# Query blocks 2, 3, 6 and 7 of the expert layers: other buffers, another load order, and four instead of six row gathers ahead

## The chip, the cores and the metric

The program runs on one core of one Trainium2 chip. The metric is the device time of one execution in microseconds (us). Engines are named as in the profile: PE (TensorE), DVE (VectorE), ACT (ScalarE), POOL (GpSimd) and SP (SyncE, which here only issues transfers). A block, a gather or one head's keys are 128 x 2048 f32, that is 1,048,576 bytes, called 1 MB or one unit below.

## What is computed

Two transformer blocks one after the other, 256 tokens of width 1024, in f32. The first block has two layers, and each ends in the same expert stage, which is where the change lies:

```
def peer_ffn(h, w_query, sub_keys, expert_u, expert_v):
    q = (ht @ w_query).reshape(T, Hh, 2, PEER_HALF)          # 256 x 1024 @ 1024 x 2048
    scores = jnp.einsum('thpd,hpkd->thpk', q, sub_keys)
    s_top, i_top = lax.top_k(scores, K)                      # 16 of 128, twice
    cand = s_top[:, :, 0, :, None] + s_top[:, :, 1, None, :]
    best, pos = lax.top_k(cand, K)                           # 16 of 256
    expert_idx = ...; gates = softmax(best)
    u = expert_u[idx]                                        # 8 heads x 16 picks a token
    a = gelu(einsum('tkd,td->tk', u, xb)) * gates
    return einsum('tk,tkd->td', a, expert_v[idx])
```

For each token and each of 128 picks one row of `u` and one of `v` (1024 f32 each) are read from a table in memory. The picks depend on the data, so these rows are gathered.

## The kernel before

**The stages.** Retention mixer, expert layer 0, gated mixer (`sgu`), expert layer 1, then the second block (hybrid attention, memory attention, MLP). Everything is written out by hand: each engine runs its own list in program order, and the lists are tied by semaphores.

**Weight blocks.** Every weight matrix is cut into blocks of 128 x 4 x 512. SP issues their loads one after the other in the order of one long list (`for i in range(limit)`), most of them into a ring of `R = 4` buffers. Before a load SP waits until PE has used the block that held the buffer last (`wait_block_free`: `w_used`, or `sum_ready` where that block was the last of a product). While SP waits, all that is behind it in the list waits too. ACT makes the rounded high part of a block (`ring_high`, L2117) and DVE the rest (`ring_low`, L1293), in place over the raw block; PE multiplies the three terms.

**The query product** of an expert layer has eight blocks, here called b0 to b7: b0, b1 for column group 0, b2, b3 for group 1, b4, b5 for group 2, b6, b7 for group 3. b8, b9 are the first two of the next matrix (`sgu_w_in` in layer 0, `w_kv_mem` in layer 1). b4 and b5 have buffers of their own (`early_scores`, `early_mod`), the others go through the ring. So b6 and b7 wait for b0 and b1 to be used, b8 and b9 for b2 and b3. Groups 0 and 1 are multiplied before the first pick is applied; groups 2 and 3 are cut into pieces and put between the picks.

**The gathers.** Two tiles of 128 tokens, 128 picks each: 256 gathers a layer, picks s = 0 to 255. One gather (POOL, L569) brings for each of 128 tokens the row pair u, v of its pick into a slot of 8 KB a partition. There are nine slots: 0 to 5 in the arena (`uv0` to `uv5`, from offset 8192 on, 2048 apart), 6 and 7 in the upper half of `ring_high` (`uv_high`), 8 is `spare`. `pick_slots` deals them out: eight at first, slot 5 from pick 68 on (`OPEN_AT`). Pick s waits until the pick that had its slot before is used (`uv_used`). DVE then multiplies u with the token (`dot`, L1705), ACT makes the gate a diagonal matrix (`p_diag`), PE adds the gated v (L1025).

**The first picks.** `choose_first` gives the first eight indices of head 0 early (`first_idx_ready`). Slots 6 and 7 lie on high parts of b2 and b3, so POOL waits ahead of pick 6 for the product of group 1 (`sum_ready` of `("query", l, 1)`):

```
if s == 6:
    pool.wait_ge(sum_ready, SUM[("query", l, 1)] + 1)
```

POOL's list is in order, so all gathers behind pick 6 wait there too.

Of the kernel before, what the change touches and what calls it, by code (L numbers as in the profile page):

```python
# [8 lines left out]
F32 = mybir.dt.float32  # L9
F32R = mybir.dt.float32r  # L10
# [14 lines left out]
RET_HEADS = 4  # L25
# [9 lines left out]
PICKS = PEER_HEADS * TOPK  # L35
# [7 lines left out]
R = 4  # L43
RH = 4
BN = 512
BK = 4
# [7 lines left out]
OPEN_AT = 68  # L54
# [45 lines left out]
def pick_slots():  # L100


    opened = 2 * [{0: (0, 1, 2, 3, 4, 8, 6, 7), OPEN_AT: (5,)}]
    at, before, held = [], [], {}
    for l in range(2):
        free, row, old = collections.deque(), [], []
        for s in range(TT * PICKS):
            free.extendleft(reversed(opened[l].get(s, ())))
            slot = free.popleft()
            free.append(slot)  # L110
            row.append(slot)
            old.append(held.get(slot))
            held[slot] = l * TT * PICKS + s
        at.append(row)
        before.append(old)
    return at, before
# [69 lines left out]
def two_blocks(nc, w, out):  # L186
# [10 lines left out]
    SMALL = small_in_order()  # L197
# [18 lines left out]
    limit = len(blocks)  # L216
    kv_first = first_block_of[("mem_kv", 0)]
    query_first = [first_block_of[("query", l, 0)] for l in range(2)]
    paired = {i for l in range(2) for i in range(query_first[l] + 4, query_first[l] + 10)} | set(range(kv_first, kv_first + 10))
    high_at = [i % 2 if i in paired else i % RH for i in range(limit)]  # L220
    early = {query_first[l] + 4 + e: R + e for l in range(2) for e in range(2)}
    raw_at, in_ring = [], 0
    for i in range(limit):
        raw_at.append(early[i] if i in early else in_ring % R)
# [9 lines left out]
    with ExitStack() as ctx:  # L234
        def sb(name, shape, dt=F32):
            return ctx.enter_context(nc.sbuf_tensor(name, shape, dt))

        def sem(name):
            return ctx.enter_context(nc.semaphore(name))
# [10 lines left out]
        ring_low = nc.alloc_sbuf_tensor_at("ring_low", [P, R, BK, BN], F32R, offset=ring_base)  # L250
        high_base = (nc.sbuf_base + 31) // 32 * 32
        ring_high = sb("ring_high", [P, RH, BK, BN], F32R)
        spare = sb("spare", [P, 2, D])
        x = sb("x", [P, TT, D])
        gain_base = (nc.sbuf_base + 31) // 32 * 32
# [35 lines left out]

        early_raw = [at("early_scores", 6144, BK, BN), nc.alloc_sbuf_tensor_at("early_mod", [P, BK, BN], F32, offset=mod_base + 12288)[:]]
        early_low = [at("early_scores_low", 6144, BK, BN, dt=F32R), nc.alloc_sbuf_tensor_at("early_mod_low", [P, BK, BN], F32R, offset=mod_base + 12288)[:]]
        raws = [ring[:, i] for i in range(R)] + early_raw
        raw_lows = [ring_low[:, i] for i in range(R)] + early_low

# [48 lines left out]
        small = [ctx.enter_context(nc.psum_tensor(f"small{i}", [P, 512], F32)) for i in range(2)]  # L345


        w_in = [sem(f"w_in{i}") for i in range(R + 2)]
        w_high, w_low, w_low_pool = sem("w_high"), sem("w_low"), sem("w_low_pool")
        t_high = sem("t_high")  # L350
        w_used = sem("w_used")
# [2 lines left out]
        small_ready = sem("small_ready")  # L354
# [25 lines left out]
        dot_ready, diag_ready, uv_used = sem("dot_ready"), sem("diag_ready"), sem("uv_used")  # L380
# [110 lines left out]
        def norm_count(n, t):  # L491
            return TT * NORM[n] + t + 1
# [18 lines left out]
        @block.sync  # L511
        def _(sp):
            sp.dma_start(col[:], w["cols"]).then_inc(c_in, 16)
            for k in range(KD):
                sp.dma_start(first_rows[k].rearrange("p a d -> p (a d)"), w["ada_w"][0, k * P:(k + 1) * P, 0:2 * D]).then_inc(first_in[k], 16)
                if k == 1:
                    sp.dma_start(x[:], w["x"][0].rearrange("(t p) d -> p t d", p=P)).then_inc(x_in, 16)
                    sp.dma_start(ident[:], w["ident"]).then_inc(cst_in, 16)
            for i in range(limit):
                if raw_before[i] is not None:  # L520
                    wait_block_free(sp, raw_before[i])
                if i in early:
                    l = query_first.index(i - 4 - early[i] + R)
                    if early[i] == R:
                        sp.wait_ge(sum_ready, SUM[("sgu_out", 1) if l else ("ret_out", 1)] + 1)
                    else:
                        sp.wait_ge(h_ready, h_count(1 + 2 * l, 1, 1))
                if i in behind_rows:
                    sp.wait_ge(dot_ready, behind_rows[i])
                sp.dma_start(raws[raw_at[i]], blocks[i]).then_inc(w_in[raw_at[i]], 16)  # L530
                for j in loaded_after[i]:
                    if j == 6 * KD:
                        sp.wait_ge(x_ready, norm_count(2, 1))
                    load_ada(sp, j)
            for t in range(TT):
                sp.wait_ge(out_ready, t + 1)
                sp.dma_start(out[0, t * P:(t + 1) * P, :], f_out[:, t, :]).then_inc(out_done, 16)
            sp.wait_ge(out_done, 16 * TT)
# [3 lines left out]
        def _(pool):  # L542
# [3 lines left out]
            def gathers(l):  # L546

                for s in range(TT * PICKS):
                    if s == 0:
                        pool.wait_ge(first_idx_ready, l + 1)  # L550
                    elif s == TOPK // 2 or s % TOPK == 0:
                        pool.wait_ge(idx_ready, l * UNITS + s // TOPK + 1)
                    if s == OPEN_AT:
                        pool.wait_ge(small_ready, SMALL[("scores", l, 3, TT - 1)] + 1)
                        if l == 0:
                            pool.dma_start(s_wsT, w["ws_turned"]).then_inc(ws_in, 16)
                    if l == 1 and s == 5 * TOPK:
                        load_gain(mix_gain, w["g_mix_2"], mix_gain_in)
                        pool.dma_start(b_mask, w["att_mask"]).then_inc(hyb_in, 16)
                        pool.dma_start(b_ga, bc(w["g_attn_out_2"].rearrange("(a d) -> a d", a=1), [P, 512])).then_inc(hyb_in, 16)  # L560
                    if l == 1 and s == PICKS + TOPK:
                        pool.wait_ge(dot_ready, TT * PICKS + PICKS)
                        load_gain(final_gain, w["norm_final"], gain_in[0])
                    if s == 6:
                        pool.wait_ge(sum_ready, SUM[("query", l, 1)] + 1)
                    if SLOT_BEFORE[l][s] is not None:
                        pool.wait_ge(uv_used, SLOT_BEFORE[l][s] + 1)
                    k = s % PICKS
                    nc.gpsimd.indirect_dma_start(uv_rows[SLOT[l][s]].rearrange("p a d -> p (a d)"), None, experts,  # L569
                                                 bass.IndirectOffsetOnAxis(ap=p_idx[:, k:k + 1], axis=0))\  # L570
                        .then_inc(landed[l, s][0], 16)
# [2040 lines left out]
```

## Time and profile before

| | |
|---|---|
| time, median of 3 runs | 2240.28 us (2239.32 to 2241.86) |
| the profiled execution | 2242.59 us, its span 2240.8 us |
| PE busy | 1973.3 us (88%) |
| DVE busy | 1561.9 us (70%) |
| ACT busy | 1029.4 us (46%) |
| POOL busy | 623.7 us (28%) |
| moved by DMA | 761.24 MB, mean 340 GB/s |
| of it by the gathers' queue (q0) | 548.94 MB |

The span is the time from the first to the last instruction of the profiled execution; the time also holds the 1.8 us around it. Busy shares are means over stages with different limits. "DMA share" is the mean busy share of the 16 DMA engines. An engine's "idle" is followed by what ended it.

### The profile page before, as it was taken

What the parts mean: (1) busy time and instruction counts of PE and PEld (TensorE: products, weight loads), DVE (VectorE), ACT (ScalarE), POOL (GpSimd) and SP (SyncE); (2) the same over time, 40 slices, a digit from 0 to 9 for tenths busy, and PEclk for the clock granted to TensorE, in tenths of its full rate; (3) what the DMA queues carried; (4) which work ended last, traced back from release to release, by engine and by line L of the source; (5) the groups of instructions that cost most, each with busy time, mean ns of one, the idle gap of its engine ahead of it and who ended that gap; (6) DMA issues with size and microseconds to landing.
All of it is one profiled execution on the core that took longest, in us unless ns stands there. A gap on an engine that the chain in (4) does not pass through costs nothing. (4 is left out here: it accounts for less than half of the span.)

```text
span 2240.8 us, 24068 instructions
## 1 busy us (share of the span) xinstructions
PE 1973.3 (88%) x8100; PEld 1242.8 (55%) x8100; DVE 1561.9 (70%) x2944; ACT 1029.4 (46%) x2171; POOL 623.7 (28%) x552
## 2 busy tenths in 40 slices
PE   6999899977778888899999998888888889999998
PEld 5886755422223233479876544334343326888987
DVE  7977787767667775578878767676777655565654
ACT  4344355544444444344444644444455444544443
POOL 1000154534434444100005444444445430200000
PEclk9999999999998999999999999999989999999999
DMA  8895799999999999886669999999999995333553
GB/s 333 302 330 204 283 421 421 421 422 421 421 421 421 422 421 421 326 320 230 231 256 417 418 421 420 421 421 421 421 408 421 422 421 199 127 141 132 188 188 132
DMA packets 112396, 761.24 MB, mean 340 GB/s; under 512 B 12832, under 2 KB 13600, under 8 KB 26128
## 3 DMA queue, kind: packets, MB, share of 16 engines
q0 software_dynamic: 76480, 548.94, 59.1%
q1 hardware_dynamic: 34832, 207.74, 25.2%
q10 hardware_dynamic: 960, 3.01, 0.4%
q8 instruction: 64, 1.05, 0.2%
q14 instruction: 60, 0.49, 0.1%
HBM read 758.60 MB, written 1.05 MB: 339 GB/s over the span
## 5 line engine op out<-in xcount | busy, mean ns | idle before, releaser
L1025 PE MATMUL pair<-uv,p_diag 128*128 128x512 f32 x1352 | 648.5, 614 | 114.1 <-ACT p_diag L2325 112.1
L1705 DVE CUSTOM_DVE_ANT_0 uv<-uv,p_h 128x1024 f32<-128x1024 f32 x338 | 413.5, 1224 | 241.0 <-DMA uv<-in_peer_uv,p_idx 239.9
L569 POOL DMA_INDIRECT uv<-in_peer_uv,p_idx x338 | 396.8, 1174 | 506.8 <-PE pair L1025 372.9
L1025 PEld LDWEIGHTS pair<-uv,p_diag 128*128 128x128 f32 x1352 | 241.7, 192 | 492.8 <-ACT p_diag L2325 276.0
L1293 DVE TENSOR_TENSOR ring_low<-ring,ring_high 128x2048 fp32r<-128x2048 f32 x143 | 326.7, 2298 | 118.3 <-ACT ring_high L2117 116.9
L2317 ACT ACTIVATE p_act<-p_dot 128x1 f32<-128x1 f32 x512 | 103.5, 202 | 627.1 <-DVE p_dot L1705 625.0
L2117 ACT ACTIVATE ring_high<-ring 128x2048 fp32r<-128x2048 f32 x144 | 272.1, 1908 | 185.3 <-DMA ring<-in_ret_w_in 47.7
L721 PE MATMUL pair<-hT_high,ring_high 128*128 128x256 f32 x960 | 287.7, 300 | 2.3 <-DVE ring_low L1293 2.3
L1025 PE MATMUL pair<-uv_high,p_diag 128*128 128x512 f32 x464 | 233.0, 634 | 53.1 <-ACT p_diag L2325 49.5
L721 PE MATMUL pair<-hT_low,ring_high 128*128 128x256 f32 x960 | 272.3, 284 | 0.0
L721 PE MATMUL pair<-hT_high,ring_low 128*128 128x256 f32 x896 | 254.2, 284 | 0.0
L2325 ACT ACTIVATE p_diag<-ident,p_w 128x128 f32<-128x128 f32 x512 | 205.7, 402 | 17.6 <-PE pair L1025 0.6
L1705 DVE CUSTOM_DVE_ANT_0 uv_high<-uv_high,p_h 128x1024 f32<-128x1024 f32 x116 | 142.1, 1225 | 86.2 <-DMA uv_high<-in_peer_uv,p_idx 85.9
L721 PEld LDWEIGHTS pair<-hT_high,ring_high 128*128 128x128 f32 x960 | 184.8, 193 | 14.0 <-issue 12.2
L1025 PEld LDWEIGHTS pair<-uv_high,p_diag 128*128 128x128 f32 x464 | 86.4, 199 | 187.2 <-ACT p_diag L2325 103.7
L721 PEld LDWEIGHTS pair<-hT_low,ring_high 128*128 128x128 f32 x960 | 184.8, 192 | 8.3 <-issue 8.2
L569 POOL DMA_INDIRECT uv_high<-in_peer_uv,p_idx x116 | 129.7, 1118 | 198.7 <-PE pair L1025 171.7
L2321 ACT ACTIVATE p_w<-p_act,p_gate 128x1 f32<-128x1 f32 x512 | 150.7, 294 | 50.1 <-ACT p_act L2317 1.9
L721 PEld LDWEIGHTS pair<-hT_high,ring_low 128*128 128x128 f32 x896 | 172.4, 192 | 0.0
L1025 PE MATMUL pair<-spare,p_diag 128*128 128x512 f32 x232 | 122.5, 654 | 32.2 <-ACT p_diag L2325 32.2
L1705 DVE CUSTOM_DVE_ANT_0 spare<-spare,p_h 128x1024 f32<-128x1024 f32 x58 | 71.0, 1224 | 50.1 <-DMA spare<-in_peer_uv,p_idx 49.9
L673 PE MATMUL pair<-ring_high,hT_high 128*128 128x512 f32 x240 | 97.0, 404 | 5.2 <-DVE ring_low L1293 3.6
(409 smaller groups left out, 2664.7 us busy)
## 6 DMA issues: line engine op xcount, KB each, us to landing
ada<-in_ada_w SPq DMA_DIRECT2D x50, 512.0 KB, 5.9
ring<-in_ret_w_in SPq DMA_DIRECT2D x24, 1024.0 KB, 6.0
ring<-in_sgu_w_in SPq DMA_DIRECT2D x24, 1024.0 KB, 7.6
ring<-in_w_up SPq DMA_DIRECT2D x16, 1024.0 KB, 4.7
ring<-in_w_down SPq DMA_DIRECT2D x16, 1024.0 KB, 4.8
mod<-in_ada_w SPq DMA_DIRECT2D x30, 512.0 KB, 6.0
ring<-in_peer_w_query SPq DMA_DIRECT2D x12, 1024.0 KB, 7.4
ring<-in_sgu_w_out SPq DMA_DIRECT2D x12, 1024.0 KB, 5.1
```

The source lines that it names most:

```text
L569: nc.gpsimd.indirect_dma_start(uv_rows[SLOT[l][s]].rearrange("p a d -> p (a d)"), None, experts, bass.IndirectOffsetOnAxis(ap=p_idx[:, k:k ...
L673: mm = nc.tensor.matmul(acc[:, t, :], a, b[:, k, :], start=(first and k == 0 and j == 0), stop=(last and k == BK - 1 and j == 2))
L721: mm = nc.tensor.matmul(acc[:, nt // 2, nt % 2 * S:(nt % 2 + 1) * S], a[:, k, n_tile], b[:, kk, :], start=(kk == 0 and nt % 2 == 0 and j = ...
L1025: mm = nc.tensor.matmul(acc[:, half, :], p_diag[:, n % DIAGS, :], v[:, half * 512:(half + 1) * 512], start=(k == 0), stop=(k == PICKS - 1))
L1293: did(V.tensor_tensor(raw_lows[raw_at[i]], raws[raw_at[i]], ring_high[:, high_at[i]].bitcast(F32), ALU.subtract), w_low, low_by_dve.index( ...
L1705: V.tensor_tensor_reduce(out=u, in0=u, in1=p_h[:, s // PICKS, :], scale=1.0, scalar=0.0, op0=ALU.mult, op1=ALU.add, accum_out=p_dot[:, n % ...
L2117: did(A.activation(ring_high[:, high_at[i]], raws[raw_at[i]], ACT.Copy), w_high, i + 1)
L2317: did(A.activation(p_act[:, d:d + 1], p_dot[:, d:d + 1], ACT.Gelu_apprx_tanh))
L2321: did(A.activation(p_w[:, d:d + 1], p_act[:, d:d + 1], ACT.Copy, scale=p_gate[:, s % PICKS:s % PICKS + 1]))
L2325: did(A.activation(p_diag[:, n % DIAGS, :], ident[:], ACT.Copy, scale=p_w[:, d:d + 1]), diag_ready, n + 1)
```

## The change

It does four things, in both expert layers:

- b2 gets the buffer of slot 8 (`early_spare`), b3 that of arena slot 3 (`early_row`, offset 14336), instead of ring buffers.
- b6 and b7 stay in the ring, but take the buffers that b2 and b3 had, which the last blocks of the matrix ahead free. SP's list is put in another order: b2, b3, b6, b7, b4, b5 in layer 0, b2, b6, b7, b3, b4, b5 in layer 1.
- b8 and b9 now follow b0 and b1 in the ring, no longer b2 and b3.
- The slots are dealt as 0, 1, 2, 4, 3, 8, 6, 7, and POOL's wait for the product of group 1 stands ahead of pick 4 instead of pick 6, since slots 3 and 8 now hold b3 and b2 until then.

```
-    opened = 2 * [{0: (0, 1, 2, 3, 4, 8, 6, 7), OPEN_AT: (5,)}]
+    opened = 2 * [{0: (0, 1, 2, 4, 3, 8, 6, 7), OPEN_AT: (5,)}]
...
-    early = {query_first[l] + 4 + e: R + e for l in range(2) for e in range(2)}
+    early = {query_first[l] + b: R + e for l in range(2) for e, b in enumerate((4, 5, 2, 3))}
+    in_order = list(range(limit))
+    for l, order in enumerate(((2, 3, 6, 7, 4, 5), (2, 6, 7, 3, 4, 5))):
+        in_order[query_first[l] + 2:query_first[l] + 8] = [query_first[l] + b for b in order]
...
+        early_raw += [nc.alloc_sbuf_tensor_at("early_spare", [P, BK, BN], F32, offset=spare_base)[:], at("early_row", 14336, BK, BN)]
+        early_low += [nc.alloc_sbuf_tensor_at("early_spare_low", [P, BK, BN], F32R, offset=spare_base)[:], at("early_row_low", 14336, BK, BN, dt=F32R)]
...
-            for i in range(limit):
+            for i in in_order:
                 if raw_before[i] is not None:
                     wait_block_free(sp, raw_before[i])
                 if i in early:
-                    l = query_first.index(i - 4 - early[i] + R)
-                    if early[i] == R:
+                    l = int(i >= query_first[1])
+                    if early[i] == R or early[i] == R + 3 and l:
                         sp.wait_ge(sum_ready, SUM[("sgu_out", 1) if l else ("ret_out", 1)] + 1)
-                    else:
+                    elif early[i] == R + 2 and l:
+                        sp.wait_ge(uv_used, TT * PICKS)
+                    elif early[i] == R + 3:
+                        sp.wait_ge(small_ready, SMALL[("ygT", 2 * RET_HEADS - 1)] + 1)
+                    elif early[i] == R + 1:
                         sp.wait_ge(h_ready, h_count(1 + 2 * l, 1, 1))
...
-                    if s == 6:
+                    if s == 4:
                         pool.wait_ge(sum_ready, SUM[("query", l, 1)] + 1)
```

SP's list at the query blocks of layer 0, before (b0 to b2, b3, b4, b5, b6, b7, b8, b9; a number behind a name only tells buffers apart):

```order
L530 DMA ring<-in_peer_w_query 128x2048 [waits w_used] x3
L530 DMA ring<-in_peer_w_query 128x2048 [waits sum_ready]
L530 DMA early_scores_85<-in_peer_w_query 128x2048 [waits sum_ready]
L530 DMA early_mod_86<-in_peer_w_query 128x2048 [waits h_ready]
L530 DMA ring<-in_peer_w_query 128x2048 [waits w_used]
L530 DMA ring<-in_peer_w_query 128x2048 [waits sum_ready]
L530 DMA ring<-in_sgu_w_in 128x2048 [waits w_used]
L530 DMA ring<-in_sgu_w_in 128x2048 [waits sum_ready]
```

The same place after (b0 and b1, b2, b3, b6, b7, b4, b5, b8, b9):

```order
L540 DMA ring<-in_peer_w_query 128x2048 [waits w_used] x2
L540 DMA early_spare_89<-in_peer_w_query 128x2048
L540 DMA early_row_90<-in_peer_w_query 128x2048 [waits small_ready]
L540 DMA ring<-in_peer_w_query 128x2048 [waits w_used]
L540 DMA ring<-in_peer_w_query 128x2048 [waits sum_ready]
L540 DMA early_scores_85<-in_peer_w_query 128x2048 [waits sum_ready]
L540 DMA early_mod_86<-in_peer_w_query 128x2048 [waits h_ready]
L540 DMA ring<-in_sgu_w_in 128x2048 [waits w_used]
L540 DMA ring<-in_sgu_w_in 128x2048 [waits sum_ready]
```

b2 and b3 no longer wait for a ring buffer, and b6 and b7 stand where they stood.

POOL's list at the start of the gathers of layer 0, before (picks 0 to 8):

```order
L569 DMA uv0_92<-in_peer_uv,p_idx_117 128x2048 [waits first_idx_ready]
L569 DMA uv1_93<-in_peer_uv,p_idx_117 128x2048
L569 DMA uv2_94<-in_peer_uv,p_idx_117 128x2048
L569 DMA uv3_95<-in_peer_uv,p_idx_117 128x2048
L569 DMA uv4_96<-in_peer_uv,p_idx_117 128x2048
L569 DMA spare<-in_peer_uv,p_idx_117 128x2048
L569 DMA uv_high0_98<-in_peer_uv,p_idx_117 128x2048 [waits sum_ready]
L569 DMA uv_high1_99<-in_peer_uv,p_idx_117 128x2048
L569 DMA uv0_92<-in_peer_uv,p_idx_117 128x2048 [waits uv_used,idx_ready]
```

And after:

```order
L579 DMA uv0_96<-in_peer_uv,p_idx_121 128x2048 [waits first_idx_ready]
L579 DMA uv1_97<-in_peer_uv,p_idx_121 128x2048
L579 DMA uv2_98<-in_peer_uv,p_idx_121 128x2048
L579 DMA uv4_100<-in_peer_uv,p_idx_121 128x2048
L579 DMA uv3_99<-in_peer_uv,p_idx_121 128x2048 [waits sum_ready]
L579 DMA spare<-in_peer_uv,p_idx_121 128x2048
L579 DMA uv_high0_102<-in_peer_uv,p_idx_121 128x2048
L579 DMA uv_high1_103<-in_peer_uv,p_idx_121 128x2048
L579 DMA uv0_96<-in_peer_uv,p_idx_121 128x2048 [waits uv_used,idx_ready]
```

The wait for `sum_ready` has moved up by two picks, and slot 3 behind it.

## Rows read from the trace of the kernel before

**Rows 1.** The page, costliest groups: DVE's dots on arena slots

```profile
L1705 DVE CUSTOM_DVE_ANT_0 uv<-uv,p_h 128x1024 f32<-128x1024 f32 x338 | 413.5, 1224 | 241.0 <-DMA uv<-in_peer_uv,p_idx 239.9
```

**Rows 2.** Windows inside both gather phases; last three columns: PEclk, DMA share, GB/s

```profile
340.00:640.00 300.00, 250.84 (x646) 105.84 (x645) 213.43 (x542) 138.90 (x391) 135.31 (x121) 0.98 1.01 421
1223.00:1640.00 417.00, 358.39 (x1099) 177.81 (x1098) 298.78 (x723) 200.16 (x531) 182.28 (x162) 0.97 1.01 421
```

**Rows 3.** POOL's timeline, layer 0, gathers 0 and 6: start, length, then idle before

```profile
268.69 1.03 POOL L569 DMA_INDIRECT uv<-in_peer_uv,p_idx  x1 [76.30 <-DVE p_idx L1668]
...
290.90 1.46 POOL L569 DMA_INDIRECT uv_high<-in_peer_uv,p_idx  x1 [10.44 <-PE pair L721]
```

**Rows 4.** SP's queue, layer 0: b1; b2; b6 and b7; b8 and b9

```profile
240.13 0.33 SPq L530 DMA_DIRECT2D ring<-in_peer_w_query  x1
...
255.27 0.33 SPq L530 DMA_DIRECT2D ring<-in_peer_w_query  x1
...
276.85 1.29 SPq L530 DMA_DIRECT2D ring<-in_peer_w_query  x2
284.90 6.09 SPq L530 DMA_DIRECT2D ring<-in_sgu_w_in  x2
```

**Rows 5.** Windows around the start of the gathers, layer 0

```profile
247.00:253.00 6.00, 6.00 (x21) 4.77 (x21) 4.49 (x5) 3.75 (x7) 0.00 (x0) 0.75 0.00 0
267.00:270.00 3.00, 3.00 (x27) 3.00 (x27) 2.86 (x10) 2.63 (x2) 1.03 (x1) 1.00 0.05 22
270.00:280.00 10.00, 10.00 (x86) 10.00 (x86) 9.93 (x14) 2.78 (x3) 8.76 (x5) 1.00 0.96 353
280.00:286.00 6.00, 6.00 (x53) 6.00 (x52) 5.29 (x24) 5.67 (x7) 0.47 (x1) 1.00 1.01 423
286.00:311.00 25.00, 22.05 (x88) 12.73 (x87) 22.38 (x63) 13.00 (x34) 13.97 (x9) 0.94 1.01 423
```

**Rows 6.** SP's queue and ACT's keys load, layer 1: b1; b2; b6 and b7

```profile
1153.71 0.33 SPq L530 DMA_DIRECT2D ring<-in_peer_w_query  x1
1161.87 0.33 SPq L530 DMA_DIRECT2D ring<-in_peer_w_query  x1
1162.49 0.34 ACTq L2271 DMA_DIRECT2D p_keysT<-in_keys_turned  x1
...
1184.12 1.29 SPq L530 DMA_DIRECT2D ring<-in_peer_w_query  x2
```

**Rows 7.** POOL's timeline, layer 1: two loads (1 MB, 0.5 MB), gathers 0 and 6

```profile
1167.39 0.76 POOL L631 DMA_DIRECT2D m_h<-in_mem  x1 [124.21 <-DVEq L1408]
1168.15 0.55 POOL L632 DMA_DIRECT2D m_row_gain<-in_g_mem  x1
1176.04 0.99 POOL L569 DMA_INDIRECT uv<-in_peer_uv,p_idx  x1 [7.34 <-DVE p_idx L1668]
...
1198.17 1.55 POOL L569 DMA_INDIRECT uv_high<-in_peer_uv,p_idx  x1 [10.35 <-PE pair L721]
```

**Rows 8.** Windows around the start of the gathers, layer 1

```profile
1160.00:1162.00 2.00, 2.00 (x11) 1.65 (x10) 1.87 (x3) 1.88 (x6) 0.00 (x0) 1.00 0.04 16
1162.00:1164.00 2.00, 2.00 (x11) 1.65 (x10) 1.20 (x2) 1.52 (x7) 0.00 (x0) 1.00 0.53 102
1164.00:1178.00 14.00, 11.94 (x94) 10.70 (x93) 12.24 (x34) 10.23 (x13) 2.97 (x4) 1.00 1.01 421
1178.00:1181.00 3.00, 3.00 (x27) 3.00 (x26) 3.00 (x2) 0.00 (x0) 2.69 (x2) 1.00 0.97 325
1181.00:1198.00 17.00, 17.00 (x143) 16.93 (x142) 16.16 (x52) 10.25 (x15) 5.90 (x4) 1.00 1.01 423
```

**Rows 9.** DVE's dots of picks 11 and 255, layer 0, and a window at its end

```profile
313.60 1.22 DVE L1705 CUSTOM_DVE_ANT_0 uv<-uv,p_h 128x1024 f32<-128x1024 f32 x1 [0.70 <-DMA uv<-in_peer_uv,p_idx]
...
928.54 1.22 DVE L1705 CUSTOM_DVE_ANT_0 uv<-uv,p_h 128x1024 f32<-128x1024 f32 x1 [1.22 <-DMA uv<-in_peer_uv,p_idx]
...
924.00:928.00 4.00, 3.47 (x8) 1.06 (x6) 2.08 (x4) 1.42 (x6) 0.00 (x0) 1.00 0.10 43
```

More of the change, by code:

```diff
@@ L252, in two_blocks @@
         ring_high = sb("ring_high", [P, RH, BK, BN], F32R)
+        spare_base = (nc.sbuf_base + 31) // 32 * 32
         spare = sb("spare", [P, 2, D])
@@ L345, in two_blocks @@
         small = [ctx.enter_context(nc.psum_tensor(f"small{i}", [P, 512], F32)) for i in range(2)]
-        w_in = [sem(f"w_in{i}") for i in range(R + 2)]
+        w_in = [sem(f"w_in{i}") for i in range(R + 4)]
         w_high, w_low, w_low_pool = sem("w_high"), sem("w_low"), sem("w_low_pool")
```

## The prediction

> **What bounds the kernel now.** I read the page's busy shares first (PE 88%) and did not stop there, since the change lies in the two expert stages only. The page's group of the dots comes next: DVE sat idle 241.0 us before them, and 239.9 us of that ended with a gather's landing [rows 1]. The windows then say what the gathers wait for: deep inside both phases the 16 DMA engines are busy all the time (share 1.01) and move 421 GB/s [rows 2]. So from the first gather to the last dot an expert stage lasts as long as its bytes: one unit (1.049 MB) costs 1.049/0.421 = 2.49 us. What is moved ahead of the gathers into time in which DMA is idle is gained at that price, and every microsecond in which DMA runs dry after the first gather is lost in full, as all 256 gathers and the mixer behind them shift with it. The rest of the kernel sees nothing of the change: b8 and b9 are only consumed much later, and b10 waits for its old condition.
>
> **What the change moves ahead, layer 0.** DMA moves nothing from 247 to 253 us and nearly nothing from 267 to 270 [rows 5]. Before, b2 is issued at 255.27, although b1 is out at 240.13; b6 and b7 follow at 276.85 to 278.14 and b8 and b9 from 284.90 on, all four inside the bounded stretch [rows 4]. After, b2 and b3 have no ring buffer to wait for and are issued right behind b1, at about 240.5 and 241; they land in the idle time. b6 and b7 take the places of b2 and b3 (255 to 258), in front of the first gather at 268.69 [rows 3]. b8 and b9 take the places of b6 and b7. Of four units only two are left behind the first gather: 2 x 2.49 = 5.0 us less to move.
>
> **Layer 1.** Here SP's new order lets only b2 go ahead (issued behind b1, 1153.71, instead of 1161.87 [rows 6]); b3 comes behind b6 and b7. DMA is idle from 1160 to 1162 (16 GB/s) and half used to 1164, and is full from there without a break [rows 8]. b2 needs 2.5 us, of which 1.9 us stand free in that window and the rest in the ones before it. One unit is gained: 2.5 us.
>
> **What it costs: the dry spell.** Before, six gathers are out ahead of POOL's wait for the product of group 1; that wait ends at 290.90 in layer 0 and 1198.17 in layer 1, each time released by PE's product [rows 3, 7]. Neither time should move: PE runs through the stretch without a gap (10.00 of 10.00 and 6.00 of 6.00 us, clock 1.00 [rows 5]), and the blocks that this product needs only come earlier. After, only four gathers are out until then. When does DMA run dry?
>
> Layer 0: from 270 us there are 4 gathers, b8 and b9, 6 units = 6.29 MB. The windows move 3.53 MB to 280 and 2.54 MB more to 286 [rows 5]; the last 0.22 MB take 0.5 us: dry at 286.5. The wait ends 4.4 us later.
>
> Layer 1: from 1162 there are b6, the keys, b7, b3, b4, b5, 1.5 units for `m_h` and `m_row_gain`, 4 gathers, b8 and b9 (b6 and b7's old places at 1184.12 [rows 6]): 13.5 units = 14.16 MB. The windows move 0.20, 5.89 and 0.98 MB to 1181 [rows 8]; the last 7.08 MB at 423 GB/s take 16.7 us: dry at 1197.7, 0.5 us ahead of the wait's end.
>
> Two unknowns are added. **x**, from the release of POOL to full flow: no row shows a restart of this kind. The nearest is the first gather: issued at 268.69, and the windows show nothing before 270, so at least 1.3 us [rows 3, 5]. At most: the 3.53 MB that the first ten microseconds moved are 8.4 us at full rate, as if it had begun at 271.6, so 2.9 us. I take the middle, 2.1: the second train has a full POOL list behind it, but an empty DMA in front. **s**, by how much the slowest engines are behind the mean one and therefore run dry later (a gather lands when its slowest engine has it): at least 0. At most: 16 units, the first 12 gathers and b6 to b9, are moved by 311.3 on the mean (3.53 + 2.54 + 25 x 0.423 MB to 311, then 0.3 us), and the dot of pick 11 gets its rows at 313.60 [rows 9], so 2.3 us. I take 1.0, since part of that is the landing itself.
>
> Loss of layer 0: 4.4 + x - s; of layer 1: 0.5 + x - s, and never below 0. **The sum:** (4.4 + x - s) + (0.5 + x - s) - 3 x 2.49 = 2(x - s) - 2.6, with x = 2.1 and s = 1.0: layer 0 +0.5, layer 1 -0.9, together **-0.4 us**. Against the profiled time of 2242.59 (span 2240.8 and 1.8 around it) that is 2242.2; the median of the runs shown is 2.3 below the profiled one, so the forecast is 2240.28 - 0.4 = **2239.9 us**.
>
> The Trainium skill, "DMA: Bandwidth & Descriptors", section on the anatomy of a SWDGE DMA, puts a fixed 2.0 us on each such transfer and says that most of it is the write receipt after the last byte, and its specifications give about 1 us to the first byte. By 1.0 for x the sum would be -2.6 us, an estimate from that page; the row with at least 1.3 decides for me.
>
> **Small costs.** The extra entries of SP's list (0.3 us each) stand where SP waits anyway. Dots 4 to 7 come later than before, and with them the choice of head 1's picks, which are cut between those dots; gather 16 needs these. Twelve gathers (4 to 15) are 30 us of transfers from about 293 on, so DMA is covered to 322. Gather 16 follows the use of pick 8, whose dot came ahead of pick 11's at 313.60 [rows 9], so an estimate for its old time is 315; it may come 5 us later for nothing, and I expect 1 to 2. Hence nothing. b2 and b3 right behind b1 (layer 0): if they took bandwidth from b1 rather than queue behind it, ACT's high part of b1, and the norm behind it in ACT's list, would be up to two units, 5 us, late. I take 0, since they go out on the same queue after it; without that cover it is a term of up to +5 in layer 0, and in the range only in part.
>
> **The rivals.**
>
> (a) *The slow engines set the pace from the start; faster.* The window at the end of layer 0 has a DMA share of 0.10 from 924 to 928, under two of 16 engines, and the last dot waits for them until 928.54 [rows 9]. So two engines are some 8 us behind at the end. If they already were so at 286, they would not run dry, and the three units would be gained in full: -7.5 us, 2232.8. For a gain of over 4.5 us, s must be 1.4 above x (layer 1's loss is then 0, and 4.4 + x - s - 7.5 = -4.5), with x = 2.1 an s of 3.5. Against it: pick 11's dot allows 2.3 at most. The same page, section "Latency and other measured facts", says that engines 7 and 15 are usually slower than the rest, above all for gathers of POOL's kind; the trace agrees that it is about two engines, and what counts here is only how far behind they are at the start.
>
> (b) *The restart is slow; slower.* The first ten microseconds of the first train ran at 353 instead of 421 GB/s after the first gather had met an empty DMA [rows 5], which is what gather 4 will meet. If the restart costs 5 us instead of 2, the sum is 2(5 - 1) - 2.6 = +5.4, 2245.7. With s = 1 it decides (over +4.5) from x = 4.6 on. For it: layer 1's dip to 325 GB/s at its first gathers [rows 8]. Against: gathers 6 and 7 followed a wait as well, though not an empty DMA, and the flow stayed at 423 [rows 5].
>
> (c) *DMA is never dry, or the wait's end moves.* If PE's product ended 2 us earlier since b2 and b3 are in early, layer 0 would stand at 0.5 - 2 = -1.5 and layer 1 at -2.5, -4.0 in all, 2236.3. Against: PE has no gap there. And if the change did not do what it says, b2 and b3 going out no earlier, b6 to b9 would all be behind the first gather in layer 0, DMA dry only at 291.5, and the loss and gain of both layers about nothing: 2240.5. Against: b2 waits for nothing in layer 0, and the transposes that b3 waits for stand ahead, in PE's list, of the use that lets b1 go at 240.13 [rows 4].
>
> **How the numbers follow.** A measurement of this kernel tells from about 0.2% on, 4.5 us. Forecast (sum within 4.5 us): 0.62; its own range, x = 1.3 with s = 2.3 (-1.6 and -2.5, since layer 1's loss stops at 0) to x = 2.9 with s = 0 (+3.2), is 2236.2 to 2243.5. Rival (a) and the good half of (c), faster by over 0.2%: 0.20. Rival (b) with the bad half of (c), slower: 0.18. The range is widened a little on both sides for these: 2235.0 to 2245.5.
>
> **What would show it.** In the profile after: in layer 0 b2 and b3 issued by 242 us and landing in the idle stretch around 247; four gathers from 268.7, then POOL idle until 290.9 (and 1198), released by PE's product; a window with DMA near 0 from about 287 to 292 and one of 1 to 2 us near 1198; pick 11's dot 0 to 1 us later than 313.6 in layer 0 and the last dot at 928.5 to 929.5; layer 1's gather phase about 1 us shorter. I would be wrong if POOL's wait ended at another time than 290.9, if DMA stayed full through it, if flow took over 4 us to return, or if the stretch before 268.7 moved.

## The result, and the profile after

The changed kernel takes 2243.58 us (2240.21 to 2246.63), the one before 2240.3 us in the same series (2237.28 to 2244.22). The ratio is 1.0013 with a 95% interval of 1.0007 to 1.0019, which is 1.6 to 4.3 us more, 2.9 in the middle. The forecast was 0.4 us less, a gain that this measurement would not have told from nothing. So it missed on the sign, by 3.3 us (2.9 + 0.4); 2243.58 lies inside the range.

The profiled execution of the changed kernel took 2241.86 us, less than the profiled one of before. The page:

```profile
span 2240.0 us, 24070 instructions
PE 1971.6 (88%) x8100; PEld 1242.5 (55%) x8100; DVE 1561.3 (70%) x2944; ACT 1029.6 (46%) x2171; POOL 621.1 (28%) x552
L1715 DVE CUSTOM_DVE_ANT_0 uv<-uv,p_h 128x1024 f32<-128x1024 f32 x338 | 413.5, 1224 | 243.1 <-DMA uv<-in_peer_uv,p_idx 241.8
```

Busy times are as before; the dots' idle behind gathers is 1.9 us more (241.8, [rows 1] had 239.9). A span of one execution is too coarse here: the mixer between the two layers alone took between 261.3 and 267.5 us in my profiles, without any edit to it. I therefore measure each expert layer by itself, from the start of its first dot to the start of its last one. DVE's timeline before (start, length, then idle before):

```profile
285.96 1.23 DVE L1705 CUSTOM_DVE_ANT_0 uv<-uv,p_h 128x1024 f32<-128x1024 f32 x1
...
1193.31 1.22 DVE L1705 CUSTOM_DVE_ANT_0 uv<-uv,p_h 128x1024 f32<-128x1024 f32 x1
1860.24 1.23 DVE L1705 CUSTOM_DVE_ANT_0 uv<-uv,p_h 128x1024 f32<-128x1024 f32 x1 [1.22 <-DMA uv<-in_peer_uv,p_idx]
```

And after:

```profile
285.52 1.23 DVE L1715 CUSTOM_DVE_ANT_0 uv<-uv,p_h 128x1024 f32<-128x1024 f32 x1
930.20 1.23 DVE L1715 CUSTOM_DVE_ANT_0 uv<-uv,p_h 128x1024 f32<-128x1024 f32 x1 [1.22 <-DMA uv<-in_peer_uv,p_idx]
1192.29 1.23 DVE L1715 CUSTOM_DVE_ANT_0 uv<-uv,p_h 128x1024 f32<-128x1024 f32 x1
1859.50 1.23 DVE L1715 CUSTOM_DVE_ANT_0 uv<-uv,p_h 128x1024 f32<-128x1024 f32 x1 [1.23 <-DMA uv<-in_peer_uv,p_idx]
```

Layer 0 went from 928.54 - 285.96 = 642.58 us [rows 9] to 930.20 - 285.52 = 644.68, **+2.10**; layer 1 from 666.93 to 667.21, **+0.28**. It comes from one profiled execution of each kernel. Where an experiment leaves a layer as it was, it moved by up to 0.3 us. Where two kernels have the same code for a layer, it differed by 0.4 to 0.6 us (the change against e1 and e2 below; e9 against e10 in layer 0), and once, at another clock, by 1.5. So the +0.28 of layer 1 can't be told from nothing.

SP's queue and POOL's timeline in layer 0, after, against [rows 3, 4]:

```profile
240.49 0.33 SPq L540 DMA_DIRECT2D ring<-in_peer_w_query  x1
240.86 0.43 SPq L540 DMA_DIRECT2D early_spare<-in_peer_w_query  x1
241.33 0.43 SPq L540 DMA_DIRECT2D early_row<-in_peer_w_query  x1
...
268.26 1.03 POOL L579 DMA_INDIRECT uv<-in_peer_uv,p_idx  x1 [75.73 <-DVE p_idx L1678]
...
290.46 1.47 POOL L579 DMA_INDIRECT uv<-in_peer_uv,p_idx  x1 [13.87 <-PE pair L731]
```

The windows of layer 0 after (busy of PE, PEld, DVE, ACT, POOL, then PEclk, DMA share, GB/s), against [rows 5]:

```profile
247.00:253.00 6.00, 6.00 (x23) 4.84 (x22) 4.64 (x6) 3.75 (x7) 0.00 (x0) 0.80 0.63 236
270.00:286.00 16.00, 16.00 (x137) 16.00 (x136) 15.22 (x37) 8.46 (x9) 5.98 (x3) 1.00 1.00 371
286.00:288.00 2.00, 2.00 (x19) 2.00 (x19) 1.97 (x9) 0.79 (x3) 0.00 (x0) 1.00 0.49 197
288.00:292.00 4.00, 4.00 (x24) 2.97 (x23) 3.93 (x16) 1.73 (x7) 1.47 (x1) 1.00 0.00 0
292.00:304.00 12.00, 10.27 (x36) 5.20 (x34) 7.95 (x19) 4.76 (x13) 9.63 (x8) 1.00 0.94 350
304.00:340.00 36.00, 32.98 (x105) 17.06 (x104) 28.45 (x72) 15.99 (x48) 17.67 (x15) 0.91 1.01 423
```

b2 and b3 are out right behind b1 and fill the stretch that stood at 0. DMA then runs dry, moves nothing from 288 to 292, and after POOL's release at 290.46 moves 350 GB/s for twelve microseconds and not 421. Those 12 us move 4.20 MB, 10.0 us of full flow, so it is as if full flow had begun at 294.0: **3.5 us after the release**. The end of the first train is read the same way: the last 2 x 197 GB/s = 0.39 MB are 0.9 us of full flow behind 286, so it is as if full flow had lasted to 286.9. From there to 294.0 DMA idles, 7.1 us, and two units (5.0 us) are saved: +2.1. That the dots show +2.10 is partly luck, since the same code in e1 has +1.63 and two things are left out that about cancel. Up to 286.9 DMA had moved some 0.3 MB (0.7 us) less than before at the same distance from the first gather. And the slowest engines, which a gather waits for, stop later than the mean one: DMA still moves 131 GB/s from 287 to 287.5 and 16 to 288, up to 1.1 us behind 286.9.

The same for layer 1, against [rows 7, 8]: POOL's timeline, then the windows.

```profile
1175.02 0.99 POOL L579 DMA_INDIRECT uv<-in_peer_uv,p_idx  x1 [7.59 <-DVE p_idx L1678]
...
1197.83 0.94 POOL L579 DMA_INDIRECT uv<-in_peer_uv,p_idx  x1 [14.47 <-PE pair L731]
...
1196.00:1199.00 3.00, 3.00 (x14) 1.80 (x13) 2.93 (x12) 1.65 (x6) 0.94 (x1) 1.00 0.25 101
1199.00:1204.00 5.00, 5.00 (x16) 2.37 (x15) 2.44 (x6) 1.76 (x4) 4.01 (x4) 1.00 0.91 313
```

101 x 3 us is 0.30 MB or 0.7 us of full flow: dry at 1196.7. 313 x 5 us is 1.57 MB or 3.7 us: as if full from 1200.3, 2.5 us after the release. DMA idles 3.6 us. What is saved is about the one unit (2.5 us) that I had. The windows from 1150 to the first gather of each kernel, before and then after:

```profile
1150.00:1176.04 26.04, 23.98 (x140) 20.33 (x139) 20.88 (x41) 15.49 (x24) 1.31 (x3) 1.00 0.84 323
1150.00:1175.02 25.02, 23.22 (x138) 20.14 (x137) 20.64 (x41) 14.46 (x23) 1.31 (x2) 1.00 0.94 375
```

That is 9.38 MB against 8.41, 0.97 MB more, 2.3 us. The mean engine thus loses 3.6 - 2.3 = 1.3 us. The dots show +0.28, and +0.84 for the same code in e2. The slowest engines explain a part, as they stop late here too: DMA still moves 33 GB/s from 1197.5 to 1198 and 16 to 1198.5, at least 1.3 us behind 1196.7.

### The profile page after: what moved, and what is told of

It is laid out like the page before. It is cut to its first block and busy times, and to the rows that moved or that the text cites. A ratio compares the mean times of both kernels' runs of the same rounds, so it can differ in the third digit from the quotient of the medians.

```text
span 2240.0 us, 24070 instructions
## 1 busy us (share of the span) xinstructions
PE 1971.6 (88%) x8100; PEld 1242.5 (55%) x8100; DVE 1561.3 (70%) x2944; ACT 1029.6 (46%) x2171; POOL 621.1 (28%) x552
## 5 line engine op out<-in xcount | busy, mean ns | idle before, releaser
L1715 DVE CUSTOM_DVE_ANT_0 uv<-uv,p_h 128x1024 f32<-128x1024 f32 x338 | 413.5, 1224 | 243.1 <-DMA uv<-in_peer_uv,p_idx 241.8
L1303 DVE TENSOR_TENSOR ring_low<-ring,ring_high 128x2048 fp32r<-128x2048 f32 x139 | 317.9, 2298 | 117.2 <-ACT ring_high L2127 116.2
L2127 ACT ACTIVATE ring_high<-ring 128x2048 fp32r<-128x2048 f32 x140 | 264.5, 1908 | 175.9 <-DMA ring<-in_ret_w_in 43.6
L731 PE MATMUL pair<-hT_high,ring_low 128*128 128x256 f32 x832 | 236.0, 284 | 0.0
L731 PEld LDWEIGHTS pair<-hT_high,ring_low 128*128 128x128 f32 x832 | 160.1, 192 | 0.0
```

Of the source, the lines that this page charges most:

```text
L731: mm = nc.tensor.matmul(acc[:, nt // 2, nt % 2 * S:(nt % 2 + 1) * S], a[:, k, n_tile], b[:, kk, :], start=(kk == 0 and nt % 2 == 0 and j = ...
L1303: did(V.tensor_tensor(raw_lows[raw_at[i]], raws[raw_at[i]], ring_high[:, high_at[i]].bitcast(F32), ALU.subtract), w_low, low_by_dve.index( ...
L1715: V.tensor_tensor_reduce(out=u, in0=u, in1=p_h[:, s // PICKS, :], scale=1.0, scalar=0.0, op0=ALU.mult, op1=ALU.add, accum_out=p_dot[:, n % ...
L2127: did(A.activation(ring_high[:, high_at[i]], raws[raw_at[i]], ACT.Copy), w_high, i + 1)
```

## The experiments

The stages' columns are the change of the two layers' times against before, measured as above. Times are compared on one chip; the time of before there was 2240.38 us for e1 to e4, 2240.59 for e5 to e8 and 2240.06 for e9 and e10.

| kernel | layer 0 | layer 1 | time, us | ratio to before, 95% |
|---|---|---|---|---|
| the change | +2.10 | +0.28 | 2243.58 | 1.0013 [1.0007, 1.0019] |
| e1 layer 0 only | +1.63 | +0.22 | 2242.31 | 1.0006 [0.9996, 1.0015] |
| e2 layer 1 only | +0.28 | +0.84 | 2241.88 | 1.0010 [1.0001, 1.0019] |
| e3 the wait only | +3.62 | +1.41 | 2245.79 | 1.0023 [1.0011, 1.0034] |
| e4 three ahead | +4.29 | +2.60 | 2248.32 | 1.0040 [1.0026, 1.0054] |
| e5 wait split | -1.94 | -3.97 | 2235.15 | 0.9974 [0.9965, 0.9983] |
| e6 before, wait split | +0.10 | +0.22 | 2240.44 | 0.9995 [0.9986, 1.0003] |
| e7 five ahead | +0.78 | -0.25 | 2240.30 | 1.0002 [0.9993, 1.0011] |
| e8 b9 held | +3.63 | +2.60 | 2247.95 | 1.0029 [1.0017, 1.0042] |
| e9 five ahead, wait split | -2.65 | -2.55 | 2233.79 | 0.9973 [0.9963, 0.9984] |
| e10 mixed | -2.21 | -2.49 | 2236.74 | 0.9983 [0.9974, 0.9992] |

The theory after the result: the loads that go ahead are gained, and the dry spell ahead of POOL's release, with a restart slower than I took it, costs a little more than they bring. The rivals: the loss lies in the new slots or in SP's order, not in the wait; or it lies in the late choice of head 1's picks.

**e1 and e2: one layer each.** The edit for e1 (e2 has it the other way round, with `l == 1`):

```
-    opened = 2 * [{0: (0, 1, 2, 4, 3, 8, 6, 7), OPEN_AT: (5,)}]
+    opened = [{0: (0, 1, 2, 4, 3, 8, 6, 7), OPEN_AT: (5,)}, {0: (0, 1, 2, 3, 4, 8, 6, 7), OPEN_AT: (5,)}]
...
-                    if s == 4:
+                    if s == (4 if l == 0 else 6):
```

The second layer also loads b2 to b7 in their old order, b2 and b3 through the ring.

> The change in expert layer 0 alone; layer 1 as before. Measured is the stretch from the first to the last dot of a layer (before: 642.58 us in layer 0, 666.93 in layer 1; the changed kernel: 644.68 and 667.21). Theory A (two gathers fewer ahead let DMA run dry until PE's product ends, and that dry spell costs more than the two units moved ahead give back): layer 0 at 644.7 (+2.1), layer 1 at 666.9 (0), time about +2. Rival B (the loss is not in the stretch at the start of the gathers but elsewhere, such as the later choice steps or other positions in the ring): the +2.1 would not stay with layer 0, or the time would move without it.

> The change in expert layer 1 alone. Theory A: layer 0 at 642.6 (0), layer 1 at 667.2 (+0.3): the dry spell there is half as long as in layer 0 and pays for the one unit moved ahead; time about 0 to +0.5. Rival B: more than +1 in layer 1, or the sum of this run and the one for layer 0 alone differs from the changed kernel by over 1 us.

Measured +1.63 in layer 0 alone and +0.84 in layer 1 alone, and +0.22 and +0.28 in the layers left as they were: layer 0 loses by itself, layer 1 by little more than the 0.6 us by which equal code differs, and nothing beyond that is carried from one to the other. The times are too close together to tell more than that both halves are slower, if anything.

**e3: the wait alone.** Loads, buffers and slots of before; only the wait moves from pick 6 to pick 4.

```
-                    if s == 6:
+                    if s == 4:
```

> The kernel before with nothing but POOL's wait moved from pick 6 to pick 4: no load moves. Theory A: seven units are left from 270 us to the release at 290.9 in layer 0 (four gathers, b6, b7, b8), DMA is dry from about 289 and b9, issued at 290.7, starts the flow again: about +3 in layer 0 and +2 in layer 1, +5 in all, since nothing is gained against it. Rival C (a gather fewer ahead costs nothing, the loss of the changed kernel comes from the moved loads): 642.6 and 666.9, time 0.

The stages lose 3.6 and 1.4 us, the time 5.4. So the wait by itself is what costs, without any new slot or order. The windows of e3 show the dry spell too, although b6 and b7 lie behind the first gather as well here:

```profile
288.00:292.00 4.00, 4.00 (x19) 2.52 (x18) 3.93 (x17) 2.42 (x7) 2.07 (x2) 1.00 0.45 143
292.00:304.00 12.00, 8.89 (x32) 4.63 (x31) 6.57 (x18) 3.93 (x12) 8.85 (x8) 1.00 0.98 387
```

Beside the change it says one thing more. The units moved ahead were meant to bring 7.5 us, and on top of e3 they bring 5.0 - 2.4 = 2.6: most of what is moved ahead only makes the dry spell longer.

**e4: three gathers ahead.** On the changed kernel:

```
-                    if s == 4:
+                    if s == 3:
```

> The changed kernel with the wait one pick earlier still, ahead of pick 3, so that one unit less is out during the dry spell. Theory A: the dry spell grows by a full unit in both layers: 644.7 + 2.5 = 647.2 and 667.2 + 2.5 = 669.7, time +5 against the changed kernel, about +8 against before. Rival C: no more than +1.

Against the change, layer 0 loses 2.2 us more and layer 1 2.3, nearly a unit (2.49) each. Once DMA is dry at the release, the end of a layer is the release, plus the restart, plus the gathers that are behind the wait; each gather more behind it costs nearly its own length. Its windows show the dry spell grown to nearly 8 us and the flow behind it no slower (408; the release is at 289.40 here, 1.06 us earlier than in the change):

```profile
284.00:292.00 8.00, 8.00 (x51) 6.33 (x51) 6.95 (x26) 3.88 (x11) 2.29 (x2) 1.00 0.09 15
292.00:304.00 12.00, 8.55 (x29) 4.75 (x28) 7.41 (x18) 3.73 (x12) 7.83 (x8) 0.86 0.98 408
```

**e5: the dry spell taken away.** Slot 8 holds b2 and slot 6 lies on b2's high part, so both come free when b2 is used, before the product is complete. On the changed kernel, picks 4 and 5 get these two and wait for b2 alone; slot 3 (b3) goes to pick 6:

```
-    opened = 2 * [{0: (0, 1, 2, 4, 3, 8, 6, 7), OPEN_AT: (5,)}]
+    opened = 2 * [{0: (0, 1, 2, 4, 8, 6, 3, 7), OPEN_AT: (5,)}]
...
                     if s == 4:
+                        wait_block_free(pool, query_first[l] + 2)
+                    if s == 6:
                         pool.wait_ge(sum_ready, SUM[("query", l, 1)] + 1)
```

> The changed kernel, slots dealt as 0, 1, 2, 4, 8, 6, 3, 7: slots 8 and 6 hold b2 and its high part, so picks 4 and 5 wait only for b2's use (about 284.5 us), and the wait for the whole product of group 1 stands ahead of pick 6 again. All moved loads stay. Theory A (the dry spell is what eats the gain): six gathers are out by 290 us, eight units are left from 270, DMA stays full to 291 and beyond; layer 0 at about 638 (5 below before), layer 1 at about 664.5 (2.5 below), time about 7 us below before, 2233. Rival B or C: no more than 2 us below the changed kernel.

POOL's timeline in e5, gathers 4, 5 and 6, and the windows:

```profile
285.47 0.93 POOL L581 DMA_INDIRECT spare<-in_peer_uv,p_idx  x1 [8.11 <-PE pair L733]
286.70 1.70 POOL L581 DMA_INDIRECT uv_high<-in_peer_uv,p_idx  x1 [0.30 <-issue]
291.22 1.55 POOL L581 DMA_INDIRECT uv<-in_peer_uv,p_idx  x1 [2.82 <-PE pair L733]
...
270.00:286.00 16.00, 16.00 (x137) 16.00 (x136) 15.35 (x35) 8.31 (x9) 6.98 (x5) 1.00 0.95 348
286.00:304.00 18.00, 17.48 (x83) 11.24 (x82) 16.97 (x49) 8.81 (x26) 13.04 (x9) 1.00 0.98 369
304.00:340.00 36.00, 33.26 (x120) 17.98 (x118) 27.15 (x69) 17.97 (x48) 19.16 (x17) 1.00 1.01 421
```

The same loads ahead, the same slots, and the stages take 5.9 us less than before, 8.3 less than with the change. The first rival falls here: the new slots and SP's order are in e5 too. The second doesn't, since e5 takes the late choice away as well. DVE writes head 1's picks (`p_idx`) at 308.23 in e5, at 308.37 before and at 311.53 in the change. The second rival falls by the change itself: gather 16, which needs these picks, goes out at 318.41 instead of 315.23, and DMA stays full from 304 to 340 (share 1.01, 423 GB/s, shown above).

But layer 0 gains 1.9 and not two units: DMA is never idle from 286 to 304, and still moves only 369 GB/s with a share of 0.98. Against 421 that is 18 us x 52 GB/s = 0.94 MB, 2.2 us, most of the second unit. Layer 1 gains 3.97, more than the 2.5 that were expected; e10 has the same code there and 2.49.

**e6: the split alone.** On the kernel before, pick 6 waits for b2's use and pick 7 for the product:

```
                     if s == 6:
+                        wait_block_free(pool, query_first[l] + 2)
+                    if s == 7:
                         pool.wait_ge(sum_ready, SUM[("query", l, 1)] + 1)
```

> The kernel before with the split wait alone: pick 6 (slot 6, on the high part of b2) waits for b2's use, pick 7 for the product. One gather goes out 5.6 us earlier, no load moves. Theory A: DMA was never dry in the kernel before, so one more gather ahead gives nothing: 642.6 and 666.9, time 0. Rival D (an earlier gather is worth something of its own): 1 to 2.5 us less in each layer.

No difference, in either layer. An earlier gather is worth nothing where DMA has work anyway; so e5's gain is the loads ahead, kept.

**e7: five ahead.** Only b2 leaves the ring and b3 stays, so one unit less is moved ahead in layer 0, and five gathers go out ahead of the wait. On the changed kernel:

```
-    opened = 2 * [{0: (0, 1, 2, 4, 3, 8, 6, 7), OPEN_AT: (5,)}]
+    opened = 2 * [{0: (0, 1, 2, 3, 4, 8, 6, 7), OPEN_AT: (5,)}]
-    early = {query_first[l] + b: R + e for l in range(2) for e, b in enumerate((4, 5, 2, 3))}
+    early = {query_first[l] + b: R + e for l in range(2) for e, b in enumerate((4, 5, 2))}
-    for l, order in enumerate(((2, 3, 6, 7, 4, 5), (2, 6, 7, 3, 4, 5))):
+    for l, order in enumerate(((2, 3, 6, 4, 5, 7), (2, 3, 6, 4, 5, 7))):
...
-                    if s == 4:
+                    if s == 5:
```

> Only b2 goes ahead (into slot 8), b3 stays in the ring, b6 follows it, and five gathers are out ahead of the wait, in both layers. b7 and b8 come where b6 and b7 came, b9 waits for group 1's product as before. Theory A: layer 0 has seven units from 270 us, dry from about 289 to 292.3, one unit gained: +0.8; layer 1 dry for about 2 us, one unit gained: -0.5; time about 0 against before. Rival C (moved loads cost): above the changed kernel.

Layer 0 +0.78, layer 1 -0.25, 0.8 above and 0.25 below before: one load ahead and one gather fewer ahead come out about even, too, as long as the wait is one wait.

**e8: a plain load at the release.** Is the slow flow behind the release a matter of gathers alone? On the changed kernel SP holds b9 back until POOL's release:

```
+                if i in (query_first[0] + 9, query_first[1] + 9):
+                    sp.wait_ge(sum_ready, SUM[("query", int(i >= query_first[1]), 1)] + 1)
```

> The changed kernel, but SP holds b9 back until group 1's product is done, so that DMA has a plain load at once when the wait ends, beside gather 4. The dry spell starts one unit (2.5 us) earlier. Theory E (the slow return of the flow in layer 0, 3.6 us instead of 2.1, belongs to gathers alone meeting an empty DMA): the plain load restarts the flow in about 1.5 us, so layer 0 is at 644.7 + 2.5 - 2.1 = 645.1. Theory F (it is in any restart): 647.2. In layer 1 by E 668.8, by F 669.7.

```profile
286.00:290.00 4.00, 4.00 (x36) 4.00 (x35) 3.93 (x17) 1.80 (x6) 0.00 (x0) 1.00 0.00 0
290.00:292.00 2.00, 2.00 (x7) 0.92 (x6) 1.97 (x8) 0.77 (x3) 1.47 (x1) 1.00 0.50 66
292.00:304.00 12.00, 9.72 (x34) 5.01 (x33) 7.45 (x19) 4.71 (x13) 8.47 (x8) 1.00 0.98 397
```

DMA is dry a unit earlier, and behind the release it moves 397 GB/s where the change had 350. Layer 0 is 1.5 us above the change, between the two expectations; layer 1 is 2.3 above it, close to theory F. The windows of the 20 us behind the release say more than these two numbers. The change in layer 0 and 1, then e8:

```profile
290.46:310.46 20.00, 15.57 (x44) 6.86 (x42) 14.10 (x38) 9.78 (x24) 13.53 (x11) 0.92 0.89 348
1197.83:1217.83 20.00, 14.07 (x43) 6.55 (x42) 14.19 (x39) 10.05 (x24) 15.29 (x11) 1.00 0.93 372
...
290.40:310.40 20.00, 15.40 (x44) 7.04 (x42) 13.63 (x35) 9.35 (x22) 11.66 (x10) 0.93 0.97 383
1204.66:1224.66 20.00, 15.13 (x42) 6.75 (x40) 12.96 (x35) 9.35 (x22) 12.74 (x11) 0.91 0.99 390
```

20 us x (1 - 348/421) = 3.5 us: by so much the bytes moved fall short of full flow. The same reading for every kernel with one wait and a dry spell (us from the release to what counts as full flow):

| kernel | b9 goes out at the release | layer 0 | layer 1 |
|---|---|---|---|
| the change | no | 3.5 | 2.3 |
| e1 (layer 0), e2 (layer 1), same code | no | 3.0 | 2.9 |
| e4 | no | 2.7 | 3.1 |
| e8 | yes | 1.8 | 1.5 |
| e3 | yes | 2.1 | 1.2 |
| e7 | yes | 1.7 | 1.9 |

With gathers alone it is 2.3 to 3.5 us, with b9 beside them 1.2 to 2.1, in both layers. So a load beside the gathers does bring the flow back sooner, though in e3 and e7 DMA was dry for a shorter time or hardly at all, which may be a part of their values. Whether it helps as a plain load, or because two units instead of one meet the empty queue, no run separates. And 3.5 against 2.3 in the change is no difference of the layers, as e1, e2 and e4 show.

**e9: five ahead and the split wait.** e7 with the waits of e5, one pick later:

```
                     if s == 5:
+                        wait_block_free(pool, query_first[l] + 2)
+                    if s == 7:
                         pool.wait_ge(sum_ready, SUM[("query", l, 1)] + 1)
```

> Only b2 goes ahead (as in the kernel with five gathers ahead), and the wait is split: pick 5 (slot 8) and pick 6 (slot 6) wait for b2's use at 284.5, pick 7 for the product, in both layers. Theory G (the flow falls below 421 GB/s not only when DMA is dry but already when less than about two units are queued, so what counts is how much is queued when the wait ends): at 291 us some three units are queued in layer 0, the flow stays at 421 and the one unit moved ahead is gained whole: layer 0 at 640.1 (-2.5), layer 1 at 664.4 (-2.5) or, as with the split wait of before, up to 1.5 lower; time -5, 2235.5. Theory A without G: the same in layer 0. If the earlier loads cost something of their own, 642 and 666.

```profile
270.00:286.00 16.00, 16.00 (x136) 16.00 (x136) 15.28 (x42) 8.79 (x11) 8.88 (x6) 1.00 1.01 401
286.00:304.00 18.00, 16.66 (x66) 9.26 (x64) 15.97 (x46) 10.63 (x26) 11.74 (x9) 1.00 1.01 423
```

One unit is moved ahead in each layer, and each layer gains it: 2.65 and 2.55 us against 2.49. DMA is full through the release, at 423 GB/s. This doesn't isolate theory G: in e9, as in the kernel before, b9 also goes out at the release. The kernel takes 2233.79 us, 6.3 us less than before and the lowest median of all; e5's interval overlaps with its own.

**e10: e9's layer 0 with e5's layer 1.**

> Layer 0 as in the kernel with one block ahead and the split wait, layer 1 as in the changed kernel with the split wait. Theory G: layer 0 at 640.1 (against 640.64 with two blocks ahead, whose second unit was lost again to the slow flow), layer 1 at 663.0; time 6 to 6.5 us below before, 2234. If a block ahead is worth its full 2.5 us in every case, layer 0 would be worse than with two blocks ahead by 2.5, 643.1.

Layer 0 came out at 640.37, as by theory G, and not at 643.1. Layer 1 was to keep e5's 3.97 us and gave 2.49, and the time is 3.3 us below before, not 6 to 6.5. The windows of e10 dip just ahead of the product's release:

```profile
1190.00:1192.00 2.00, 2.00 (x19) 2.00 (x18) 1.89 (x7) 1.98 (x2) 0.00 (x0) 1.00 1.02 418
1192.00:1194.00 2.00, 2.00 (x19) 2.00 (x18) 2.00 (x9) 1.46 (x6) 1.43 (x2) 1.00 0.57 180
1194.00:1196.00 2.00, 2.00 (x19) 2.00 (x19) 1.97 (x8) 0.81 (x3) 0.44 (x1) 1.00 0.84 266
```

In e5, with the same code in that layer, the last two stand at 422 and 426 GB/s. The dip is (2 x 241 + 2 x 155 GB/s) = 0.79 MB, 1.9 us, about the 1.5 by which the two differ. What differs is the stretch ahead. Its windows in e10 and then in e5:

```profile
1168.00:1174.00 6.00, 5.11 (x24) 4.74 (x24) 5.07 (x24) 3.27 (x4) 0.99 (x1) 0.50 1.02 424
1168.00:1174.00 6.00, 5.06 (x42) 4.85 (x43) 4.92 (x24) 3.16 (x4) 0.91 (x1) 1.00 1.02 421
```

TensorE was granted 0.50 of its clock (1.2 GHz) in e10 and 1.00 (2.4 GHz) in e5. Just ahead, from 1166 to 1168, PE had been busy for 0.65 us in e10 and 0.18 in e5, so that pause doesn't tell why only e10 lost its clock. PE got through its blocks later: the first of the two waits ends 19.34 us after the first gather in e10 (1192.26 - 1172.92) and 17.04 us after it in e5 (1190.13 - 1173.09). In those 2.3 us what is queued runs out. So e5's layer 1 is one execution at full clock, and the margin there is under 2.3 us.

**e11: four slots.** To see the flow with few gathers queued for a long time, the kernel before with four slots for the whole stage:

```
-    opened = 2 * [{0: (0, 1, 2, 3, 4, 8, 6, 7), OPEN_AT: (5,)}]
+    opened = 2 * [{0: (0, 1, 2, 3)}]
```

> The kernel before with four gather slots (0 to 3) instead of nine, so that hardly more than two gathers are queued at DMA at any time of the stage. Theory G: the windows in the middle of the stage show a DMA share near 1 and a flow well below 421 GB/s, between 300 and 400. Rival H (a shallow queue only means pauses): the flow falls in step with the share, so that the quotient of GB/s and share stays at 417 (421 over 1.01). Time above 2300 us either way.

```profile
400.00:600.00 200.00, 141.34 (x353) 58.65 (x351) 112.64 (x286) 73.13 (x205) 70.55 (x65) 0.97 0.92 335
600.00:700.00 100.00, 70.36 (x132) 24.21 (x132) 56.15 (x146) 35.22 (x105) 34.28 (x33) 0.93 0.93 344
```

One execution, 2559.95 us. The flow falls from 421 to 335 GB/s while the share falls only from 1.01 to 0.92. A full share at that efficiency would be 335/0.92 = 364 GB/s, not 421/1.01 = 417. So rival H falls: with four slots the stage pays in two ways, by pauses and by fewer bytes for a busy microsecond.

## Why the prediction was wrong

- **The bound, the mechanism and its places held.** b2 and b3 were out by 241.33 and filled the idle stretch; four gathers, then POOL idle until 290.46 and 1197.83, released by PE's product; a dry stretch behind 288; the rest of the kernel as before. One sign missed: pick 11's dot came at 315.98, 2.4 us later and not 0 to 1.
- **The step that failed is the size of x, "from the release of POOL to full flow".** I took 2.1 as the middle between 1.3 and 2.9. In the change it is 3.5 in layer 0, above my upper bound, and 2.3 to 2.5 in layer 1; over the six readings with gathers alone it is 2.9 in the mean, and every one is above 2.1. The bound came from the first gather, where b6 and b7 joined from 276.85 on, and I counted the slow stretch as a late start of one train. e5 shows that it is not only a start: with DMA never idle the flow still stays at 369 GB/s. I had taken 421 GB/s as the flow whenever the share is near 1. My own rows spoke against that, 353 GB/s at 0.96 [rows 5] and 325 at 0.97 [rows 8], and I read them as dips.
- **s, "the slowest engines":** 1.0 taken. The windows allow up to 1.1 us in layer 0 and 1.3 to 1.8 in layer 1 (the last engine's stop behind the mean dry point). Nothing here shows that 1.0 was wrong.
- **POOL's answer in layer 1.** The product ended where it had (its last matmul starts 21.6 us after the first gather, before and after), but gather 4 started 0.7 us later behind it than gather 6 had (22.81 us after the first gather against 22.13). e2, e3 and e8, with four gathers ahead as well, have the same 22.8, and e4 and e7, with three and five, have 22.1. The prediction had put this at nothing. Why it is so stays open.
- **The sum with the measured x:** layer 0: 4.4 + 3.5 - 1.0 - 5.0 = +1.9, the dots show +2.10. Layer 1: 0.5 + 0.7 + 2.4 - 1.0 - 2.5 = +0.1, the dots show +0.28, and +0.84 in e2. Together +2.0 against 2.4 by the dots, and the time went up by 2.9, with 1.6 to 4.3 in its interval. Of the 2.4 us between this and the forecast, x gives 1.7 and POOL's answer 0.7.
- **Small costs.** The late choice of head 1's picks costs nothing that lasts, as expected, though gather 16 was 3.2 us later and not 1 to 2: DMA stayed full from 304 to 340. b1 was not delayed: b8 and b9, which wait for b0 and b1 to be used, went out at 276.40, as b6 and b7 had at 276.85.
- **The rivals.** (a) fell: two engines may be 8 us behind at the end of the stage, but all had stopped by 288.0, at most 1.1 us behind the mean. (b) was right in kind, a slow restart, and too large in size (5 us). (c) fell: PE's product ended where it had.
- **The Trainium skill** ("DMA: Bandwidth & Descriptors", specifications) has about 1 us to a SWDGE transfer's first byte. I set its 1.0 aside for a row with at least 1.3. The trace of the change has more too: DMA moves nothing until 292.5, 2.0 us after POOL's gather began, and in layer 1 nothing from 1198.5 to 1199 and 66 GB/s from there to 1199.5, so 1.2 to 1.7 us. And what counts for the sum is not the first byte but when the bytes flow at full rate, 3.5 and 2.3 to 2.5 us.

What stays open: why the DMA engines move fewer bytes in a busy microsecond behind a release and with four slots. e5 and e11 show that they do, and e8 that a load beside the gathers shortens it; none shows why.

## What to carry to other kernels

A queue that never runs dry hides the start of every transfer in it, and the price of emptying it is the time to full flow, here 2.3 to 3.5 us with gathers alone, not the time to the first byte. Before loads are moved ahead of a bound queue, work out when the queue is empty against the time at which the next item may go: what goes ahead beyond that point only makes the hole longer, and each item held behind the wait costs nearly its whole length (2.2 and 2.3 us of 2.49 in e4). If a buffer is the price, split the wait so that each item waits only for the block that held its own buffer; that turned +2.9 us into -5.4, and with one load fewer moved ahead into -6.3.

## What was not expected of the hardware

- A DMA share near 1 doesn't mean full flow: 369 GB/s at 0.98 in e5 and 350 at 0.94 in the change, just behind the release; 335 at 0.92 with four slots; 421 at 1.01 with eight or nine.
- Full flow came back 2.3 to 3.5 us after the release with gathers alone, and the same code gave 3.5 and 3.0 in layer 0, 2.3 and 2.9 in layer 1.
- The low flow lasts long. In e5 it goes on to 304 us; from 294 to 298, say, it is 383 GB/s. By 298 POOL had issued six gathers (the first at 285.47) and 286 to 298 had moved some four units, so two to three were queued, with what was left at 286. POOL itself takes 1.2 to 3.1 us from one gather to the next there, against 2.49 for the bytes of one, so the queue grows slowly.
- The number of units queued alone doesn't explain the low flow. An estimate from the issues and the bytes moved: before, from 288 to 290, about two units were queued, and in the change, from 298 to 300, more than three. Yet the flow was 418 GB/s in the first window and 348 in the second, at a full share in both:

```profile
288.00:290.00 2.00, 2.00 (x19) 2.00 (x19) 1.97 (x8) 1.01 (x4) 0.00 (x0) 1.00 1.00 418
...
298.00:300.00 2.00, 1.90 (x11) 1.23 (x10) 0.65 (x2) 0.76 (x3) 1.57 (x2) 1.00 1.01 348
```
